# A round's result is spread one round later, the place matrix is built at the round's end, expert weights come in 16 KB pieces, router weights are loaded later

## The chip, the cores and the metric

One NeuronCore of a Trainium2 chip runs the whole program in one launch. The metric is the device time in microseconds of one execution. Three runs of the kernel before gave 1340.18, 1341.22 and 1343.46 us, median 1341.22. The profile is of the run of 1341.22 us, whose span from first to last instruction is 1339.4 us.

## The reference

One inference step of a two-layer decoder trunk, all in fp32, on 256 prompt tokens and 8 sample tokens (T = 264 columns in the kernel). Layer 0 mixes tokens by dilated window attention, layer 1 by causal pooling; each is followed by a mixture of experts, which is what the change is about:

```python
def moe_ffn(h, g_norm, wgr, bgr, wer, ber, wg, wu, wd):
    u = rms_norm(h, g_norm).reshape(n, d)                 # d = 1024
    gates = route(u, wgr, bgr, wer, ber)                  # (n, 16): 2 of 16 experts per token, others 0
    a = jnp.einsum('td,edf->tef', ub, wg)                 # f = 512
    c = jnp.einsum('td,edf->tef', ub, wu)
    hh = jax.nn.silu(a) * c * gb[:, :, None]
    return h + jnp.einsum('tef,efd->td', hh, wd)
```

`route` is a softmax over 4 groups, the best group, and the two best of its 4 experts. Beside this the program copies the three key and value caches (about 176 MB) from their input to their output tensors, shifted by one token, by DMAs from DRAM to DRAM.

## The kernel before

All activations lie transposed: `hT` and `uT` hold feature chunk k (8 of 128) on the partitions and 264 tokens along the row. SyncE (SP) issues the weight loads and the cache copies ("moves", about 1 MB each) in one order written by hand; a move goes wherever the order has room. ScalarE (ACT) and GpSimd (POOL) issue small loads and stores. All waits are written out as semaphores.

**Expert rounds.** The 16 experts are taken in pairs, 8 pairs a layer; a pair takes a round, or more where an expert has over 64 tokens (`CAP`). In this data each pair takes one, so there are 16 rounds. The bounds of the loop over rounds are read from `rounds_i` (L302) at each pair, in `all_rounds` (L301 to L307), by every engine. One round on TensorE (PE), in order:
- gather: 24 matmuls (L1180, two records each) of the token-major `u_tok` by the 0/1 matrix `pick` put the chosen tokens of both experts side by side into banks 0 and 1; DVE copies bank 0 (L928), ACT bank 1 (L708) into `u_slots`;
- place: 3 matmuls (L1187) of `pick_gate` (the same matrix times the gate) by the identity give the matrix that spreads slots back over tokens; ACT copies it to `place` (L710);
- gate and up: 64 matmul records (L1197), 32 against `ring_lo` (gate), then 32 against `region_a` (up); ACT takes Silu of bank 2 (L712), DVE multiplies by bank 3 (L931);
- turning: 4 transposes of `hid_rows` (L1202), copied by DVE (L933) and ACT (L714);
- down: L1213 into banks 4 and 5, copied by ACT into `y_pair` (L717);
- spread: 8 matmuls (L1222) of `y_pair` by `place` into four banks in turn, each added to `hT` by DVE (L936).

POOL makes `pick` (L561) and `pick_gate` (L559) in turn, 12 instructions, once the place matrix of the round before has been made (`place_made`).

**Weights.** Six slots of 2 MB (gate, up, down for either expert of a pair). SP reloads gate when the round's gate matmuls are done, up after up, then one move, down after down (`next_pair`, L418 on; `expert`, L382 to L386). The loads view a weight as `(k p) f -> p k f`: a partition gets 8 rows of 2 KB each for gate and up, 4 of 4 KB each for down.

**Router.** After the norm PE computes logits (L1144), turns `uT` into token-major banks (L1151), which DVE (L865) and ACT (L700) copy to `u_tok`; DVE then picks the experts. The router's weights are loaded by ACT (L631 to L634) at the end of the qkv stage; their semaphore `consts_landed` is the one on which PE (ahead of L1048) and DVE (ahead of L785) wait before the sample tokens' attention. After prompt attention ACT issues the pool mixer's loads (L682 to L686), and its next work is the norm's square (L285), once w_o's product has been added.

## Time and profile before

| what | value |
|---|---|
| median of the runs | 1341.22 us |
| the profiled execution | 1341.22 us, span 1339.4 us |
| PE busy | 1149.8 us, 86% |
| DVE, ACT, POOL busy | 31%, 17%, 17% |
| DMA, mean rate | 345 GB/s, 462.63 MB |
| mean granted TensorE clock | 0.908 of full |
| layer 0: first gather to last spread | 602.1 to 921.3 us |
| layer 1: the same | 1013.5 to 1332.0 us |

Times within the profile are from the first instruction. A granted clock of 1.00 is 2.4 GHz, of 0.50 is 1.2 GHz. An engine name with a q is that engine's sequencer: it waits, branches, reads registers or issues DMAs while the engine itself may be idle.

### The profile page before, as it was taken

To read this page: it belongs to the slowest core of one execution; us is meant where nothing else is said; L and a number is where in the kernel's file an instruction comes from. 1 tells how busy PE (TensorE), PEld (TensorE's weight loads), DVE (VectorE), ACT (ScalarE), POOL (GpSimd) and SP (SyncE) were. 2 spreads that over 40 slices of the span, in tenths; PEclk is the share of its full clock that TensorE was granted. 3 is DMA by queue.
4 is the path that set the end of the run, shared out by engine and by line. 5 is a ranking of instruction groups with operands and counts; after the bars stand their busy time and mean duration, and the time that the engine had idled before them with its cause. 6 is when DMAs were issued, how large, how long until landed. Compare 5 with 4: busy or idle time off the path is not lost.

```text
span 1339.4 us, 15976 instructions
## 1 busy us (share of the span) xinstructions
PE 1149.8 (86%) x5409; PEld 740.9 (55%) x5410; DVE 420.2 (31%) x821; ACT 224.1 (17%) x508; POOL 222.4 (17%) x466
## 2 busy tenths in 40 slices
PE   5998799999588999739988998997557899899888
PEld 3887688778424888635444444444344444444443
DVE  3456457546511663230111110114640111011112
ACT  1221122222100442110111111111011111111110
POOL 0014204204300120022211222100004022222100
PEclk9999899999777899857999999999655999999999
DMA  9999999998899988999999899899997998989997
GB/s 379 317 410 371 381 364 362 380 394 304 280 315 394 307 293 291 372 321 321 393 387 353 328 347 351 333 354 393 359 335 257 339 351 324 351 332 351 393 351 276
DMA packets 132562, 462.63 MB, mean 345 GB/s; under 512 B 12112, under 2 KB 20192, under 8 KB 129808
## 3 DMA queue, kind: packets, MB, share of 16 engines
q1 hardware_dynamic: 118768, 440.29, 89.3%
q0 software_dynamic: 5536, 18.88, 3.8%
q10 hardware_dynamic: 8232, 3.13, 1.0%
q8 instruction: 14, 0.23, 0.1%
q14 instruction: 12, 0.10, 0.0%
HBM read 455.19 MB, written 183.41 MB: 477 GB/s over the span
## 4 chain that ended last, share of the span: by engine, by line
PE 64%; DVE 9%; issue 5%; DMA 2%; ACT 2%; POOL 1%; ACTq 1%; DVEq 0%; POOLq 0%
PE bank L1197 17%; PE bank L1180 11%; PE bank L1213 8%; PE bank L1222 4%; PE bank L1023 4%; PE bank L1067 2%; PE bank L1135 2%; DMA out_dram<-scratch 1%; DVE ring_lo L775 1%; PE bank L1094 1%; PE bank L1187 1%; PE bank L1114 1%; PE bank L280 1%; PE bank L1102 1%; PE bank L1144 1%
## 5 line engine op out<-in xcount | busy, mean ns | idle before, releaser
L1023 PE MATMUL bank<-uT,ring_lo 128*128 128x264 f32 x1152 | 272.7, 391 | 8.5 <-DVE uT L293 6.0
L1023 PEld LDWEIGHTS bank<-uT,ring_lo 128*128 128x128 f32 x1152 | 217.2, 193 | 48.4 <-issue 9.7
L1180 PE MATMUL bank<-scratch 128*128 128x128 f32 (+1 forms) x768 | 149.2, 328 | 40.4 <-POOL scratch L561 24.8
L1180 PEld LDWEIGHTS bank<-scratch 128*128 128x128 f32 (+1 forms) x768 | 113.9, 204 | 78.5 <-issue 28.1
L1197 PE MATMUL bank<-ring_lo,scratch 128*64 128x512 f32 x512 | 124.9, 645 | 0.0
L1213 PE MATMUL bank<-ring_lo,scratch 128*64 128x512 f32 x512 | 113.4, 594 | 11.4 <-DVE scratch L933 11.4
L764 DVE RECIPROCAL scratch<-scratch 128x264 f32<-128x264 f32 x48 | 86.5, 1802 | 111.1 <-ACT scratch L611 111.1
L931 DVE TENSOR_TENSOR scratch<-bank,scratch 128x512 f32<-128x512 f32 x16 | 11.1, 691 | 327.9 <-PE bank L1197 327.9
L1197 PE MATMUL bank<-region_a,scratch 128*64 128x512 f32 x512 | 112.6, 592 | 0.0
L936 DVE TENSOR_TENSOR hT<-bank,hT 128x264 f32<-128x264 f32 x128 | 55.3, 432 | 129.7 <-PE bank L1222 128.3
L1213 PEld LDWEIGHTS bank<-ring_lo,scratch 128*64 128x64 f32 x512 | 42.3, 137 | 72.2 <-issue 72.2
L544 POOL TENSOR_TENSOR small<-epsc 128x1 f32<-128x1 f32 x65 | 12.5, 193 | 403.1 <-PE bank L1187 388.6
L1197 PEld LDWEIGHTS bank<-ring_lo,scratch 128*64 128x64 f32 x512 | 38.0, 147 | 73.2 <-issue 72.9
L1197 PEld LDWEIGHTS bank<-region_a,scratch 128*64 128x64 f32 x512 | 36.6, 137 | 73.2 <-issue 73.2
L1222 PE MATMUL bank<-scratch 128*128 128x264 f32 x256 | 61.2, 392 | 0.0
L1222 PEld LDWEIGHTS bank<-scratch 128*128 128x128 f32 x256 | 47.3, 190 | 20.3 <-issue 13.0
L481 POOL COPY region_a<-scratch 128x264 f32<-128x264 f32 x48 | 24.3, 506 | 195.3 <-DVE scratch L765 194.9
L559 POOL TENSOR_SCALAR scratch<-slot_no,scratch 128x64 f32<-128x64 f32 (+1 forms) x96 | 55.8, 582 | 0.7 <-issue 0.3
L775 DVE TENSOR_TENSOR ring_lo<-ring_lo,scratch 128x1024 f32<-128x1024 f32 x24 | 42.0, 1748 | 12.7 <-POOL scratch L473 8.7
L605 ACT ACTIVATE scratch<-bank 128x264 f32<-128x264 f32 x48 | 18.7, 390 | 157.8 <-PE bank L1023 157.8
L548 POOL COPY scratch<-scratch 128x6 f32 x16 | 3.0, 189 | 245.6 <-issue 245.6
L928 DVE COPY scratch<-bank 128x512 f32<-128x512 f32 x16 | 11.1, 691 | 102.3 <-PE bank L1180 102.3
(218 smaller groups left out, 1209.2 us busy)
## 6 DMA issues: line engine op xcount, KB each, us to landing
out_dram<-in_cache_kv_w_dram SPq DMA_DIRECT2D x128, 1023.5 KB, 17.3
ring_lo<-in_w_gate_dram SPq DMA_DIRECT2D x32, 2048.0 KB, 12.9
region_a<-in_w_up_dram SPq DMA_DIRECT2D x32, 2048.0 KB, 18.0
ring_lo<-in_w_down_dram SPq DMA_DIRECT2D x32, 2048.0 KB, 17.1
ring_lo<-in_w_qkv_dram SPq DMA_DIRECT2D x18, 2048.0 KB, 16.9
out_dram<-in_cache_kv_w_dram SPq DMA_DIRECT2D x32, 1022.0 KB, 32.8
ring_lo<-in_cache_kv_w_dram POOLq DMA_DIRECT2D x24, 512.0 KB, 10.6
ring_lo<-in_cache_kv_w_dram SPq DMA_DIRECT2D x6, 2048.0 KB, 13.9
```

What stands on the lines that cost most here:

```text
L481: nc.gpsimd.tensor_copy(qk[:, g, n // KT, n % KT, :], zn[:, n % 4, :]).then_inc(zn_kept, 1)
L559: nc.gpsimd.tensor_scalar(pick_gate[0:n, b, at], slot_no[0:n, :], pair_at[0:n, 0, b, e:e + 1], pair_at[0:n, 1, b, e:e + 1], ALU.is_equal, ...
L764: chain(vec.reciprocal(zri[:, n % 2, :], zr[:, n % 2, :]))
L775: chain(vec.tensor_tensor(k_tile, k_tile, q_rep[b % 2][:, :], ALU.mult))
L936: vec.tensor_tensor(hT[:, m, :], spread_bank[m % 4][:, 0:T], hT[:, m, :], ALU.add).then_inc(spread_added, 1)
L1023: last = mm(z_bank[s % 4][:, 0:T], w[:, k, at:at + P], uT[:, k, :], start=(k == 0), stop=(k == KT - 1))
L1067: last = mm(bank[3 + a][rows, :], p_masked[:, b % 2, g, rows], slot(g)[:, at:at + 512], start=(half == 0 and g == 0 and b % 2 == 0), stop= ...
L1135: last = mm(bank[m % 2][:, 0:T], w[:, f % 4, m * P:(m + 1) * P], oT[:, f, :], start=(f == 0), stop=(f == KT - 1))
L1180: last = mm(bank[m // 4][:, m % 4 * P:(m % 4 + 1) * P], u_tok[0:sizes[b], b, m * P:(m + 1) * P], pick[0:sizes[b], b, :], start=(b == 0), s ...
L1197: last = mm(bank[2 + w][rows, :], u_slots[:, k, rows], weights[e][w][:, k, :], start=(k == 0), stop=(k == KT - 1))
L1213: last = mm(bank[4 + a][rows, :], hid[:, f, rows], weights[e][2][:, f, a * 512:(a + 1) * 512], start=(f == 0), stop=(f == FT - 1))
L1222: mm(spread_bank[m % 4][:, 0:T], y_pair[:, m * P:(m + 1) * P], place, start=True, stop=True).then_inc(spread, 1)
```

## The change

- A round's `y_pair` and `place` are no longer spread at its end. The next round of the same layer spreads them: 4 spreads (m = 0 to 3) stand between up and turning, 4 between turning and down. DVE adds the first four between its multiply and its copy of the turned rows, the others behind that copy.
- Before a layer's first round DVE sets `y_pair` and `place` to zero (the first round then spreads zeros), and after the last round PE and DVE do one more spread of 8, for which both read the count of rounds (`all_of_layer`).
- The place matmuls stand at the end of the round, behind down, and wait for all eight additions; ACT copies `place` behind `y_pair`. Bank order for spreads is 6, 7, 2, 3.
- PE no longer waits for ACT's half of `u_slots` until half of the gate matmuls are issued.
- POOL makes all of `pick` first, as soon as the round before has gathered, and `pick_gate` once its place matrix is made; each has a semaphore of its own.
- Expert weights are viewed `(p k) f -> p (k f)`: one piece of 16 KB a partition. To match, `u_tok` is dealt out in the copies from PSUM (feature 8p+k goes to chunk k), and the transposes read every fourth column of `hid_rows`.
- The router's six loads stand behind prompt attention, ahead of the pool mixer's loads on ACT, with a semaphore of their own on which PE waits ahead of the logits.

```diff
+        def dealt(b, half, n):
+            return u_tok[0:n, b, :].rearrange("t (k p) -> t k p", k=KT)[:, :, half * HD:(half + 1) * HD]
-        spread_bank = [bank[n] for n in (2, 3, 6, 7)]
+        spread_bank = [bank[n] for n in (6, 7, 2, 3)]
-        N_CONSTS = 8 + 2 * LAYERS
+        N_CONSTS = 6
+        N_ROUTER = 2 + 2 * LAYERS
-        expert_w = (w_gate.rearrange("l e (k p) f -> (l e) p k f", p=P), ...
+        expert_w = tuple(w.rearrange("l e (a p k) f -> (l e) p a (k f)", a=1, p=P) for w in (w_gate, w_up, w_down))
+        def all_of_layer(eng, layer):
+            return eng.value_load(rounds_i[0:1, ds(layer * (NP + 1) + NP, 1)], min_val=NP, max_val=MAX_ROUNDS)
...
 POOL one_round
-                pool.wait_ge(place_made, q + 1)
+                pool.wait_ge(gathered, q * 2 + 2)
...
-                        nc.gpsimd.tensor_scalar(pick_gate[0:n, b, at], ...
                         last = nc.gpsimd.tensor_scalar(pick[0:n, b, at], ...
                 last.then_inc(pick_ready, 1)
+                pool.wait_ge(place_made, q + 1)
...
+                        last = nc.gpsimd.tensor_scalar(pick_gate[0:n, b, at], ...
+                last.then_inc(pick_gate_ready, 1)
...
 ACT, behind prompt attention (moved here from the end of the qkv stage)
+            for layer in range(LAYERS):
+                dma(wr[:, layer, :, 0:NG], router_group_w[layer].rearrange("(k p) g -> p k g", p=P)).then_inc(router_landed, 16)
+                dma(wr[:, layer, :, NG:], router_expert_w[layer].rearrange("(k p) g -> p k g", p=P)).then_inc(router_landed, 16)
+            dma(brow[:, :, 0:NG], ...).then_inc(router_landed, 16)
+            dma(brow[:, :, NG:], ...).then_inc(router_landed, 16)
...
 DVE
+                for a in range(2):
+                    vec.memset(y_pair[:, a * 512:(a + 1) * 512], 0.0).then_inc(y_copied, 1)
+                vec.memset(place, 0.0).then_inc(place_ready, 1)
...
-                    vec.tensor_copy(u_tok[0:n, b, 0:D // 2], bank[2 * b][0:n, :]).then_inc(u_tok_dve, 1)
+                    vec.tensor_copy(dealt(b, 0, n), bank[2 * b][0:n, :].rearrange("t (p k) -> t k p", k=KT)).then_inc(u_tok_dve, 1)
...
 PE one_round, behind the gather
                 pe.wait_ge(slots_dve, q + 1)
-                pe.wait_ge(slots_act, q + 1)
-                for b in range(3):
-                    last = mm(bank[6][:, b * P:b * P + sizes[b]], pick_gate[0:sizes[b], b, :], ...
...
+                        if w == 0 and k == KT // 2:
+                            pe.wait_ge(slots_act, q + 1)
...
+                pe.wait_ge(y_copied, q * 2 + 2 * (layer + 1))
+                pe.wait_ge(place_ready, q + (layer + 1))
+                for m in range(4):
+                    if m == 2:
+                        pe.wait_ge(silu_ready, q + 1)
+                        pe.wait_ge(hid_rows_ready, q + 1)
+                    spread_out(m)
                 pe.wait_ge(hid_rows_ready, q + 1)
                 for f in range(FT):
-                    last = nc.tensor.transpose(..., hid_rows[:, f * P:(f + 1) * P], ident[:])
+                    last = nc.tensor.transpose(..., hid_rows[:, f::FT], ident[:])
                 last.then_inc(hid_turned, 1)
+                for m in range(4, KT):
+                    pe.wait_ge(spread_added, q * KT + (layer * KT + m - 3))
+                    spread_out(m)
...
 behind down
-                pe.wait_ge(place_ready, q + 1)
-                for m in range(KT):
-                    ...
-                    mm(spread_bank[m % 4][:, 0:T], y_pair[:, m * P:(m + 1) * P], place, start=True, stop=True).then_inc(spread, 1)
+                pe.wait_ge(pick_gate_ready, q + 1)
+                pe.wait_ge(spread_added, q * KT + (layer + 1) * KT)
+                for b in range(3):
+                    last = mm(bank[6][:, b * P:b * P + sizes[b]], pick_gate[0:sizes[b], b, :], ...
+                last.then_inc(place_made, 1)
```

## Rows read from the trace of the kernel before

**Rows 1.** The page: busy us by engine; groups: busy us, mean ns | idle before.
```profile
PE 1149.8 (86%) x5409; PEld 740.9 (55%) x5410; DVE 420.2 (31%) x821; ACT 224.1 (17%) x508; POOL 222.4 (17%) x466
...
L936 DVE TENSOR_TENSOR hT<-bank,hT 128x264 f32<-128x264 f32 x128 | 55.3, 432 | 129.7 <-PE bank L1222 128.3
...
L559 POOL TENSOR_SCALAR scratch<-slot_no,scratch 128x64 f32<-128x64 f32 (+1 forms) x96 | 55.8, 582 | 0.7 <-issue 0.3
```
**Rows 2.** Chain of waits, one round: start us, us, what ended last.
```profile
727.37 8.52 PE bank L1180 x48
736.65 1.00 PE bank L1187 x6
737.65 15.61 PE bank L1197 x64
754.09 0.67 PE bank L1202 x4
754.79 0.43 DVE scratch L933
755.46 7.09 PE bank L1213 x32
762.55 3.76 PE bank L1222 x16
766.31 1.06 issue
```
**Rows 3.** Stretches of time: us, busy of PE, PEld, DVE, ACT, POOL, clock, DMA share, GB/s.
```profile
689.01:727.37 38.36, 34.89 (x171) 17.88 (x171) 5.27 (x11) 5.73 (x8) 7.23 (x19) 1.00 0.95 360
727.37:767.37 40.00, 36.58 (x171) 18.24 (x171) 5.27 (x11) 5.73 (x8) 7.23 (x19) 0.96 0.90 340
734.67:738.08 3.41, 2.63 (x18) 1.85 (x18) 0.00 (x0) 0.99 (x2) 0.29 (x2) 1.00 1.03 410
738.08:741.50 3.42, 3.42 (x12) 0.98 (x10) 0.00 (x0) 1.28 (x1) 3.42 (x8) 0.50 1.02 407
602.11:617.18 15.07, 15.05 (x48) 11.39 (x48) 0.69 (x1) 0.00 (x0) 1.18 (x6) 0.50 1.02 343
1013.51:1028.58 15.07, 15.06 (x48) 11.39 (x48) 0.69 (x1) 0.00 (x0) 1.16 (x6) 0.50 1.02 343
```
**Rows 4.** PE's sequencer at the loop's end, L307, 762 to 768 us.
```profile
L307 PEldq ALU_OP  x1: 32/32/32, 765.0 to 765.0; - x1
```
**Rows 5.** Chain of waits, first rounds' gate and up, layers 0 and 1.
```profile
619.66 15.10 PE bank L1197 x64
1031.06 15.90 PE bank L1197 x64
```
**Rows 6.** Timeline: PE at layer 0's start, with the idle time ahead of it.
```profile
602.11 15.05 PE L1180 MATMUL bank<-scratch 128*128 128x128 f32 x48 [12.70 <-POOL scratch L561]
```
**Rows 7.** Timeline from the qkv stage's end to the sample tokens' attention.
```profile
365.81 0.77 PE L1048 MATMUL bank<-bucket_s,tabrep 32*128 32x129 f32 x2 [12.22 <-DMA brow<-in_router_expert_b_dram]
365.08 0.95 POOL L518 COPY scratch<-region_a 128x384 f32<-128x384 f32 x2 [5.88 <-DMA out_dram<-scratch]
369.23 0.36 DVE L787 TENSOR_TENSOR scratch<-scratch 128x192 f32<-128x192 f32 x1 [2.57 <-DMA scratch<-qkv_of_samples]
```
**Rows 8.** DMA queues (packets, MB, share): 538:546 us ACT's, 356:358 ACT's, 548:551.4 SP's.
```profile
q10 hardware_dynamic: 94, 0.09, 3.7%
...
q10 hardware_dynamic: 2061, 0.08, 64.4%
...
q1 hardware_dynamic: 13, 0.00, 0.2%
```
**Rows 9.** ACT's timeline behind prompt attention.
```profile
551.88 1.96 ACT L285 ACTIVATE scratch<-hT 128x2112 f32<-128x2112 f32 x1 [29.30 <-DVE hT L854]
```
**Rows 10.** Stretches: only 4 KB pieces of down, then only 2 KB pieces.
```profile
733.00:743.00 10.00, 9.22 (x42) 4.64 (x42) 0.00 (x0) 2.27 (x3) 5.21 (x12) 0.83 1.01 404
753.00:765.00 12.00, 10.42 (x49) 5.25 (x48) 2.85 (x6) 2.24 (x4) 0.00 (x0) 1.00 1.05 388
```

More of the change, by code:

```diff
@@ L385, in expert @@
                 src = src[e] if isinstance(e, int) else src[ds(e, 1)].rearrange("a p k f -> p (a k) f")
-                sp.dma_start(slot(s).rearrange("p (k f) -> p k f", k=FT if what == 2 else KT), src).then_inc(ring_full[s], 16)
+                sp.dma_start(slot(s).rearrange("p (a f) -> p a f", a=1), src).then_inc(ring_full[s], 16)
             expert(0, 0, 0)
@@ L570, in _ @@
             carry(55).then_inc(place_made, 1)
+            for n in range(2):
+                carry(52 + n).then_inc(gathered, 1)
             for layer in range(LAYERS):
@@ L924, in router, with add_spread, one_round @@
                 vec.tensor_copy(rounds_i[0:1, layer * (NP + 1):(layer + 1) * (NP + 1)], rounds_f[0:1, layer, :]).then_inc(rounds_ready, 1)
-            def one_round(q, p):
-                dve.wait_ge(gathered, q * 2 + 1)
+            def add_spread(n, half):
+                for m in range(4 * half, 4 * half + 4):
+                    dve.wait_ge(spread, n * KT + (m + 1))
+                    vec.tensor_tensor(hT[:, m, :], spread_bank[m % 4][:, 0:T], hT[:, m, :], ALU.add).then_inc(spread_added, 1)
+            def one_round(q, layer):
+                dve.wait_ge(gathered, q * 2 + 3)
                 vec.tensor_copy(u_slots[:, 0:KT // 2, :], bank[0].rearrange("p (k n) -> p k n", n=P)).then_inc(slots_dve, 1)
@@ L931, in one_round @@
                 vec.tensor_tensor(hid_rows, bank[3][:, :], silu, ALU.mult).then_inc(hid_rows_ready, 1)
+                add_spread(q + layer, 0)
                 dve.wait_ge(hid_turned, q + 1)
                 vec.tensor_copy(hid[:, 0:2, :], bank[0][:, 0:2 * P].rearrange("p (f n) -> p f n", f=2)).then_inc(hid_dve, 1)
-                for m in range(KT):
-                    dve.wait_ge(spread, q * KT + (m + 1))
-                    vec.tensor_tensor(hT[:, m, :], spread_bank[m % 4][:, 0:T], hT[:, m, :], ALU.add).then_inc(spread_added, 1)
+                add_spread(q + layer, 1)
             def experts(layer):
                 dve.wait_ge(rounds_ready, layer + 1)
-                all_rounds(dve, layer, one_round)
+                all_rounds(dve, layer, lambda q, p: one_round(q, layer))
+                end = all_of_layer(dve, layer)
+                for half in range(2):
+                    add_spread(end + layer, half)
                 vec.memset(small[:, 62:63], 0.0).then_inc(layer_added, 1)
@@ L1139, in router @@
                 pe.wait_ge(u_ready, n_norm + 1)
+                pe.wait_ge(router_landed, 16 * N_ROUTER)
                 for b in range(3):
@@ L1169, in _, with spread_out @@
                         slot(c).rearrange("p (k f) -> p k f", k=FT)) for a, b, c in SLOTS]
+            def spread_out(m):
+                mm(spread_bank[m % 4][:, 0:T], y_pair[:, m * P:(m + 1) * P], place, start=True, stop=True).then_inc(spread, 1)
             def one_round(q, p, layer):
@@ L1215, in one_round @@
                     last.then_inc(y_half, 1)
-                pe.wait_ge(place_ready, q + 1)
-                for m in range(KT):
-                    if m % 4 == 0:
-                        pe.wait_ge(y_copied, q * 2 + (m // 4 + 1))
-                    if m >= 4:
-                        pe.wait_ge(spread_added, q * KT + (m - 3))
-                    mm(spread_bank[m % 4][:, 0:T], y_pair[:, m * P:(m + 1) * P], place, start=True, stop=True).then_inc(spread, 1)
+                pe.wait_ge(pick_gate_ready, q + 1)
+                pe.wait_ge(spread_added, q * KT + (layer + 1) * KT)
+                for b in range(3):
+                    last = mm(bank[6][:, b * P:b * P + sizes[b]], pick_gate[0:sizes[b], b, :], ident[0:sizes[b], 0:sizes[b]],
+                              start=True, stop=True)
+                last.then_inc(place_made, 1)
             def experts(layer):
                 all_rounds(pe, layer, lambda q, p: one_round(q, p, layer))
+                end = all_of_layer(pe, layer)
+                pe.wait_ge(y_copied, end * 2 + 2 * (layer + 1))
+                pe.wait_ge(place_ready, end + (layer + 1))
+                for m in range(KT):
+                    if m >= 4:
+                        pe.wait_ge(spread_added, end * KT + (layer * KT + m - 3))
+                    spread_out(m)
             norm_sums(pe, 1)
```

35 lines of the change are left out of this document (16 added, 19 removed).

## The prediction

> **What bounds the kernel now.** The page comes first: TensorE is busy 1149.8 us of 1339.4 [rows 1], every other engine a third or less (of the groups under it, DVE's eight additions a round cost 0.43 us each and POOL's `pick_gate` instructions 0.58). The chain of waits then shows that in the expert rounds nearly every step from gather to gather is PE's own [rows 2]. A round with the clock at full takes 38.36 us, one in which the clock falls once 40.00 [rows 3]; In a round PE stands still four times [rows 2]: 735.89 to 736.65, until ACT has copied its half of the slots (0.76 us); 753.26 to 754.09, until DVE has multiplied (0.83); 754.76 to 755.46, until the turned rows are copied (0.70); and 766.31 to 767.37, the loop's registers (1.06). No weight load ends a wait there. DMA is not idle, though: in these two rounds its share is 0.95 and 0.90, at 360 and 340 GB/s [rows 3].
>
> The reader should look hardest at the granted clock. Right behind the first gap and the place matmuls it fell: from 734.67 to 738.08 PE is busy 2.63 us of 3.41 and the clock is 1.00, from 738.08 to 741.50 it is 0.50 [rows 3]. That happened in 5 of the 14 rounds that are not a layer's first, each time at this place, never at the loop's gap. There the dense gate matmuls come next, and the clock is back at once: 15.61 us in place of the 13.93 that is left when 40.00 - 38.36 = 1.64 are taken off, the price of such a fall. A layer's first gather shows what a gather does at half clock: 15.07 us against 8.52, the clock at 0.50 from its first to its last matmul [rows 2, 3], and it came back only inside gate and up, which took 15.10 and 15.90 us [rows 5]. So gather doesn't bring the clock back, and gate does.
>
> **The change part by part.**
>
> Slots. Gate starts when DVE's half is there, which is copied during the second half of gather; ACT's copy lies beside the first half of gate, 3.5 us. The 0.76 us become some 0.04: 0.72 x 16 rounds = -11.5 us. Bounds: 0 and 0.76 a round.
>
> Turning. Before, from the end of up to the start of down: 755.46 - 753.26 = 2.20 us, and then spread, 3.76, behind down. After: spread m 0 and 1 take 0.94 us, longer than the 0.83 in which the multiply ends, so m 2 and 3 and the transposes (about 0.54 without the wait for the first) follow without a gap; DVE adds the first four (0.43 each [rows 1]) and copies the turned rows by about 3.1 us, while m 4 to 7 keep PE until 4.3. Down starts 4.3 us behind up, where 2.20 + 3.76 = 5.96 stood: -1.66 x 16 = -26.6 us. Bounds: 0 (all waits come back) and 1.66.
>
> The loop's gap. The sequencer began the loop's end at 765.0 [rows 4], while four spreads (two records each, 0.235 us a record) were still to run in part, and gather started at 767.37, 2.3 us later; 1.26 us of that lay under spread. Behind the change the last instructions are place's six, of which four cover only some 0.8 us, so the gap is about 1.5 us, not 1.06: +0.4 x 14 = +5.6 us. Bounds: 0 and +1.2 (nothing covered).
>
> The ends. Each layer gets one more spread (3.76) and the loop's exit ahead of it, about 1.5: +5.3 x 2 = +10.5 us. Where the place matrix took 1.72 us at half clock in a first round it now takes 1.00: -1.4 us for both.
>
> POOL. Ahead of the first gather PE waits for POOL, 12.70 us [rows 6]. Of the twelve instructions there six stay ahead of it: the six of `pick_gate` go, 0.58 apiece [rows 1], -3.5 x 2 = -7.0 us. POOL is idle four fifths of the time [rows 1], and `pick` is made a whole round early. The three memsets lie beside PE's logits.
>
> Attention. PE waited 12.22 us, until 365.8, for the router's last load [rows 7], DVE with it. Without it PE is done with these matmuls early, but DVE also waits for the token stores; POOL's wait for the same ones ended at 365.08 [rows 7], or some 1 us sooner once the router's packets no longer mix in. The sample rows land earlier too, as ACT no longer issues their loads behind the router's. So what stood at 369.23 [rows 7] starts at about 364.9: -4.5 us. Bounds: 0 (the stores are the last all the same) and 12.2 (PE's whole wait).
>
> 16 KB pieces. While only 4 KB pieces went, the 16 engines moved 404 GB/s at a share of 1.01; while only 2 KB pieces went, 388 at 1.05 [rows 10]: 400 against 370 at a share of 1. The 13.6 MB of a round need about 36 us as they are, and 33 to 34 with every piece large. No load is waited for now and none will be, for a round gets no shorter than 36: 0 us. Without the larger pieces this would be at its limit. Bounds: 0, and a few us a round should 16 KB be slower, for which no row speaks.
>
> The columns of `hid_rows` are read by every fourth. No row shows a strided read by PE. The four transposes take 0.67 us [rows 2]; the near end is nothing, the far end a doubling, 0.67 x 16 = 10.7 us. I take +2, the dealing copies with it, which lie mostly beside PE. The Trainium skill (SBUF — State Buffer, the DMA port swizzle section, its note on cachelines) says that accesses which each touch a new 16-byte line pay a penalty, and every fourth fp32 is just that; by it I would take the far end, and the sum would rise by some 9 us. No row bears on it.
>
> The router's loads stand ahead of the pool mixer's on ACT. ACT is idle 29.30 us there, until w_o's product is added at 551.9 [rows 9]. Beside SP's 64 KB pieces ACT's queue gets few packets through, 94 in 8 us, and the router has over 4,000 (1024 rows by 2 loads by 2 layers). But ahead of 551.4 SP's queue runs empty, 13 packets in 3.4 us; with nothing large beside them 2,061 such packets passed in 2 us [rows 8]. As SP's weights are through sooner, that gap grows to some 8 us. +1 us for ACT's lateness; bounds 0 and the rival below.
>
> The clock. Five falls go with the first gap: -1.64 x 5 = -8.2 us. But the place matmuls, among the sparsest work of a round, now stand right ahead of its longest gap, and behind the gap comes gather, also sparse. That is together 2.5 us with little in it, where 0.76 us of idling next to the place matmuls had been enough. I expect a fall in most rounds, and now at the head of gather, which then stays at half: up to 15.07 - 8.52 = 6.55 us, 5.4 where the fall comes a little into it, and gate begins at half too, 1.2 to 2.0 us (15.10 and 15.90 less 13.9 [rows 5]). So 7.0 us a fall. In 11 of 14 rounds: +77 us. Bounds: 0 and 14 x 8.3 = 116.
>
> Sum: -11.5 - 26.6 + 5.6 + 10.5 - 1.4 - 7.0 - 4.5 + 2 + 1 - 8.2 = -40 us without new falls, +77 with them: **+37 us**. The profiled execution is the median one, 1341.22 us for a span of 1339.4, so the changed kernel comes to 1378 us. A difference within 0.3%, 4 us, can't be told from none by timing this kernel.
>
> **The rivals.**
>
> *The clock holds (faster).* The loop's gap of 1.06 us cost no clock in 14 rounds [rows 2, 3], and what is in the changed one is only 1.5. Then only the savings are left: 1341 - 40 = 1301 us, or 1310 if as many falls as before stay at their old price. Against it: a gap of 0.76 did cost the clock. For it: the same gap did not in 9 of 14. The Trainium skill (TensorE: Matmul & The Clock Gate, HAM oscillation) warns of PE idling for far longer than either gap here, and by that rule this rival is the forecast; the falls in the trace disagree with it. The point that decides is 40 / 7 = 5.7: with six falls the change gives nothing, with fewer it is faster, with more it is slower.
>
> *A few falls.* Whether a fall comes depended on the round's position, since equal rounds differed. With 3 to 8 in place of 11: 1322 to 1357 us.
>
> *The router's packets get stuck (slower, or it eats the gain).* If they haven't gone by 551 us, SP's next 23 moves share the engines with them at about 12 packets a us [rows 8]. ACT is then held in its issues, and the norm, logits and everything behind wait. Each 12 packets left over cost 1 us: 500 would cost 42 us, 1343 us with the clock holding (1301 + 42) and 1420 with the falls (1378 + 42). For it: over 4,000 packets. Against: the gap at SP and the rate in it [rows 8].
>
> *Weights are late.* Only if 16 KB pieces run below 350 GB/s; each 10% below adds 4 us a round, some 60 in all: 1361 with the clock holding. The trend from 2 to 4 KB speaks against it.
>
> **How the numbers follow.** Falls in 9 to 14 rounds: 0.60, its own range 1355 to 1400 us. A few falls: 0.15, half of it slower, a third faster. The clock holds: 0.20, 1298 to 1318. Stuck packets or late weights: 0.05. The predicted time is 1378 us; the range 1308 to 1400 takes in most of the faster case. Faster 0.26, within 0.3% 0.05, slower 0.69.
>
> **What would show it.** Right: the granted clock at 0.50 over most gathers, a mean clock well below 0.908, gathers of 13 to 15 us, and PE's idle time between gather and gate, up and turning, and turning and down gone. Wrong: gathers of 8.52 us throughout, and rounds of some 36.5. The gap behind place should be 1.3 to 1.7 us. DVE's L787 should start near 365 us; ACT's square should follow w_o's last addition within 2 us, else the router's loads held ACT. The page should count a smaller number of packets and no wait of PE for `ring_full`.

## The result and the profile after

The changed kernel takes 1273.88 us (median of 4 runs, 1272.44 to 1276.9), the kernel before 1341.58 us beside it: a ratio of 0.9497, 95% interval 0.948 to 0.9515. The forecast was 1378 us, slower, with a range of 1308 to 1400. It was wrong in its sign. Times below are medians of all runs of a kernel; a ratio leaves out a run over 1.5% above its kernel's fastest (one, in the second test).

The page after, its line of busy times (us, share of the span, instructions); [rows 1] has the one of before:

```profile
PE 1142.9 (90%) x5441; PEld 736.3 (58%) x5442; DVE 428.3 (34%) x843; ACT 224.4 (18%) x508; POOL 225.1 (18%) x484
```

PE does almost the same work in a span of 1272.0 us, not 1339.4. Where its idle time went is seen in the chain of waits of one round after (start us, us, what ended last), beside [rows 2]:

```profile
674.36 8.44 PE bank L1214 x48
682.79 13.88 PE bank L1228 x64
696.68 2.08 PE bank L1203 x8
698.76 0.47 PE bank L1240 x4
699.23 1.78 PE bank L1203 x8
701.01 7.02 PE bank L1254 x32
708.03 0.95 PE bank L1260 x6
708.99 3.05 PE bank L1214 x17
```

L1214 is gather, L1228 gate and up, L1203 spread, L1240 turning, L1254 down, L1260 place. All eight lines are PE's and each starts where the one above ends. The last two lines are the point: place ends at 708.99 and the next round's gather starts at 708.99. The loop's gap, 1.06 us in [rows 2] and forecast to become 1.5, is not there (a line "issue", as there and below, is time in which the engine waits for nothing that the profile shows). The view of stretches shows it for a whole round, and the clock with it (us, busy of PE, PEld, DVE, ACT, POOL, granted clock, DMA share, GB/s), as [rows 3]:

```profile
674.36:708.99 34.63, 34.63 (x171) 17.39 (x171) 5.15 (x11) 5.73 (x8) 7.37 (x20) 1.00 1.00 427
593.91:608.97 15.06, 15.06 (x50) 11.47 (x52) 0.69 (x1) 0.00 (x0) 4.63 (x13) 0.50 0.96 322
```

PE is busy 34.63 us of 34.63 and the clock is 1.00. PE has no gap in any other round either, but for layer 0's second, where it stands still twice for weights (0.86 us for up's, 0.77 ahead of down), and the clock is 1.00 in every round but a layer's first. No gather but a layer's first ran at half clock. That first one still takes 15.06 us (second row), as before.

Why the gap is gone is seen at PE's sequencer, L316, the loop's end, within the same round (duration in ns, then start in us); [rows 4] is the same place before:

```profile
L316 PEldq ALU_OP  x1: 32/32/32, 704.5 to 704.5; - x1
L316 PEldq MOVE  x1: 29/29/29, 706.7 to 706.7; - x1
```

It starts on the loop's registers at 704.5, 3.5 us ahead of down's end, and is through at 706.8, 2.2 us ahead of the next gather. Before, it began at 765.0, with 1.3 us of spread left. What held it there is DVE's fourth addition of that round, for which the last spread waits (start us, us; it ends at 765.00):

```profile
764.57 0.43 DVE L936 TENSOR_TENSOR hT<-bank,hT 128x264 f32<-128x264 f32 x1
```

In the changed kernel the last of the eight additions is over long before the sequencer gets to the loop's end:

```profile
701.05 0.43 DVE L952 TENSOR_TENSOR hT<-bank,hT 128x264 f32<-128x264 f32 x1
```

The 67.4 us between the two spans, by stretches: 8.2 ahead of layer 0's first gather (602.11 to 593.91), 26.6 in layer 0 (first gather to last spread, 319.2 to 292.6), 3.5 between the layers, 29.0 in layer 1 (318.5 to 289.5).

### The profile page after: what moved, and what is told of

Its sections match the earlier page's. It is cut to its first block, busy times and chain, and to the rows that moved or that the text cites. A ratio compares the mean times of both kernels' runs of the same rounds, so it can differ in the third digit from the quotient of the medians.

```text
span 1272.0 us, 16186 instructions
## 1 busy us (share of the span) xinstructions
PE 1142.9 (90%) x5441; PEld 736.3 (58%) x5442; DVE 428.3 (34%) x843; ACT 224.4 (18%) x508; POOL 225.1 (18%) x484
## 4 chain that ended last, share of the span: by engine, by line
PE 59%; DVE 7%; issue 3%; DMA 3%; ACT 1%; POOL 1%; ACTq 1%; POOLq 0%; DVEq 0%; SPq 0%
PE bank L1228 17%; PE bank L1214 11%; PE bank L1254 8%; PE bank L1203 5%; PE bank L1165 2%; PE bank L1097 2%; DMA region_a<-in_w_up_dram 2%; PE bank L1124 1%; PE bank L1132 1%; PE bank L1144 1%; PE bank L1175 1%; PE bank L285 1%; PE bank L1260 1%; PE bank L1104 1%; PE bank L1121 1%
## 5 line engine op out<-in xcount | busy, mean ns | idle before, releaser
L1214 PE MATMUL bank<-scratch 128*128 128x128 f32 (+1 forms) x768 | 149.3, 328 | 18.0 <-POOL scratch L568 18.0
L1214 PEld LDWEIGHTS bank<-scratch 128*128 128x128 f32 (+1 forms) x768 | 113.9, 204 | 50.6 <-POOL scratch L568 18.2
L1228 PE MATMUL bank<-ring_lo,scratch 128*64 128x512 f32 x512 | 117.5, 613 | 0.0
L1254 PE MATMUL bank<-ring_lo,scratch 128*64 128x512 f32 x512 | 113.4, 595 | 0.8 <-issue 0.8
L1228 PE MATMUL bank<-region_a,scratch 128*64 128x512 f32 x512 | 112.6, 592 | 0.9 <-DMA region_a<-in_w_up_dram 0.9
L553 POOL TENSOR_TENSOR small<-epsc 128x1 f32<-128x1 f32 x83 | 16.0, 195 | 387.4 <-PE bank L1260 334.8
L1228 PEld LDWEIGHTS bank<-region_a,scratch 128*64 128x64 f32 x512 | 37.0, 137 | 73.9 <-issue 73.9
L1228 PEld LDWEIGHTS bank<-ring_lo,scratch 128*64 128x64 f32 x512 | 36.3, 141 | 69.2 <-issue 67.5
L1254 PEld LDWEIGHTS bank<-ring_lo,scratch 128*64 128x64 f32 x512 | 35.8, 137 | 69.9 <-issue 69.9
L1203 PE MATMUL bank<-scratch 128*128 128x264 f32 x288 | 73.2, 397 | 1.0 <-ACT scratch L736 1.0
L952 DVE TENSOR_TENSOR hT<-bank,hT 128x264 f32<-128x264 f32 x144 | 61.8, 432 | 20.7 <-PE bank L1203 17.5
L1203 PEld LDWEIGHTS bank<-scratch 128*128 128x128 f32 x288 | 50.8, 190 | 24.3 <-issue 17.0
L794 DVE TENSOR_TENSOR ring_lo<-ring_lo,scratch 128x1024 f32<-128x1024 f32 x24 | 42.0, 1749 | 11.5 <-POOL scratch L482 7.7
```

What stands on the lines that cost most here:

```text
L794: chain(vec.tensor_tensor(k_tile, k_tile, q_rep[b % 2][:, :], ALU.mult))
L952: vec.tensor_tensor(hT[:, m, :], spread_bank[m % 4][:, 0:T], hT[:, m, :], ALU.add).then_inc(spread_added, 1)
L1203: mm(spread_bank[m % 4][:, 0:T], y_pair[:, m * P:(m + 1) * P], place, start=True, stop=True).then_inc(spread, 1)
L1214: last = mm(bank[m // 4][:, m % 4 * P:(m % 4 + 1) * P], u_tok[0:sizes[b], b, m * P:(m + 1) * P], pick[0:sizes[b], b, :], start=(b == 0), s ...
L1228: last = mm(bank[2 + w][rows, :], u_slots[:, k, rows], weights[e][w][:, k, :], start=(k == 0), stop=(k == KT - 1))
L1254: last = mm(bank[4 + a][rows, :], hid[:, f, rows], weights[e][2][:, f, a * 512:(a + 1) * 512], start=(f == 0), stop=(f == FT - 1))
```

## The experiments

Gaps and falls below are read for the 14 rounds that are not a layer's first. A fall is a drop of the granted clock from 1.00 to 0.50 in such a round; it shows as a gather, or a gate and up, above its 8.5 or 13.95 us. They are counted in the one profiled run of each kernel. "Sparse" is said of gather and place, whose matmuls are of 128 columns, "dense" of gate, up, down and the added matmuls, of 512 or 264. The letters A, B, C are the theories of the expectation above each result.

**The forecast's arrangement made true.** Ahead of place PE waits until this round's result is copied:

```diff
                 pe.wait_ge(pick_gate_ready, q + 1)
+                pe.wait_ge(y_copied, q * 2 + 2 * (layer + 2))
                 pe.wait_ge(spread_added, q * KT + (layer + 1) * KT)
```

> This kernel makes the forecast's arrangement true: before the place matmuls PE waits until ACT has copied this round's second half of down's result, so the last instructions of a round wait late and the sequencer cannot run ahead to the loop's end. Theory A (the forecast was wrong only in what lets the sequencer run ahead; its clock term would have been right with the gap there): PE stands some 0.7 us behind down, place follows, then a loop gap of 1.3 to 1.6 us, 2.2 us a round in all, +31 us over 14 rounds, and on top a fall of the clock at the head of most gathers, about 7 us each: 1274 + 31 + 77 = 1382 us, gathers of 13 to 15 us. Theory B (the clock holds anyway beside gaps of this size, the forecast's clock term was wrong by itself): the same gaps, gathers of 8.5 us throughout, about 1305 us. Theory C (the loop's end costs nothing wherever the waits stand): a gap of 0.7 us behind down only, about 1284 us.

Measured: 1411.99 us, ratio 1.055 (1.0518 to 1.0582). The chain of one round of it:

```profile
721.64 0.61 ACT scratch L734
722.25 0.12 issue
722.37 1.02 PE bank L1261 x6
723.39 1.37 issue
724.76 14.13 PE bank L1214 x48
738.89 15.96 PE bank L1228 x64
```

PE's sequencer at the same loop end:

```profile
L316 PEldq ALU_OP  x1: 32/32/32, 722.4 to 722.4; - x1
```

And the stretches of its gather and of the whole round:

```profile
724.76:738.89 14.13, 14.13 (x50) 10.75 (x52) 0.69 (x1) 1.28 (x1) 3.42 (x11) 0.54 0.86 368
724.76:769.37 44.61, 42.46 (x170) 21.95 (x171) 5.15 (x11) 5.73 (x8) 7.42 (x21) 0.81 0.73 306
```

Theory A, and more of it than forecast. The sequencer comes to the loop's end only at 722.4, as place starts; place covers 1.0 us of it and 1.37 are left. Gather then runs at a clock of 0.54. It fell in 14 rounds of 14, and a round takes 44.6 us: 34.63, 2.1 of gaps and 7.8 for the clock (one, the second of layer 1, takes 46.2). One wait in another place makes the change slower than the kernel before.

**A gap behind place alone.** Only gather waits, for ACT's copy of the place matrix:

```diff
                 pe.wait_ge(pick_ready, q + 1)
+                pe.wait_ge(place_ready, q + (layer + 1))
```

> Here only gather waits, for ACT's copy of the place matrix of the round before; the last instructions of a round do not wait, so the sequencer meets the loop's end early and the gap is that of the copy alone, some 0.6 us behind place. Theory A (run-ahead hides the loop's end, and a gap behind the place matmuls can cost the clock): gap 0.5 to 0.7 us, no loop gap added, +9 us over 14 rounds, 1283 us if the clock holds; with falls as often as behind the old gap of 0.76 us (5 of 14), now priced at 7 us, 1318 us. Theory B (clock holds beside such gaps): 1283 us and gathers of 8.5 us. Theory C (the sequencer does not hide the loop's end behind a round of its own): gap above 1.2 us, 1295 us or more.

Measured: 1323.74 us (1315.22 to 1338.08), ratio 0.9861 (0.981 to 0.9912). The profiled run is the fastest, 1315.22. It has gaps of 0.57 us in layer 0 and 0.48 in layer 1, so no loop gap was added, and 5 falls of 14. A round with and one without a fall, and the gather of the former:

```profile
673.11:708.35 35.24, 34.67 (x170) 17.38 (x171) 5.15 (x11) 5.73 (x8) 7.41 (x21) 1.00 1.01 429
708.35:749.72 41.37, 40.79 (x170) 20.96 (x171) 5.15 (x11) 5.73 (x8) 7.42 (x21) 0.83 0.84 352
708.35:721.35 13.00, 13.00 (x50) 9.82 (x52) 0.69 (x1) 1.28 (x1) 4.22 (x12) 0.60 1.01 430
```

Theory A again: half a microsecond of idling at this place costs 6 us or more when it brings a fall, and equal gaps bring it only at times. The spread of the four runs fits a number of falls that differs from run to run: the mean clock is 0.889 in the fastest and 0.875 in the slowest.

**The same gap, longer.** ACT makes two copies more ahead of that of the place matrix:

```diff
                     ac.wait_ge(place_made, q + 2)
+                    nc.scalar.activation(silu[:, 0:T], bank[6][:, 0:T], ACT.Copy)
+                    nc.scalar.activation(silu[:, T:], bank[6][:, 0:512 - T], ACT.Copy)
...
+                pe.wait_ge(place_ready, q + (layer + 1))
```

> The changed kernel; gather waits for ACT's copy of the place matrix, ahead of which ACT now copies 512 columns of the same bank elsewhere (results unused). Nothing waits ahead of place, so this is the forecast's own arrangement: one gap of its size right behind the place matmuls. The copy alone gave a gap of 0.48 to 0.57 us and 5 falls in 14; the late place gave gaps of 0.77 and 1.37 us around the place matmuls and 14 falls in 14. Theory A (a gap of this size behind place costs the clock by itself): gap 1.2 to 1.5 us, falls in 11 to 14 of 14, gathers of 13 to 15 us, 8 us a fall: 1274 + 18 + 11..14 x 8 = 1380 to 1404 us. Theory B (it needed both gaps, ahead of place and behind it): about 5 falls, 1274 + 18 + 40 = 1332 us. Theory C (the clock holds behind one gap): 1292 us.

Measured: 1378.1 us (1362.17 to 1384.75), a little under theory A's 1380 to 1404. The profiled run took 1372.1; it has gaps of 1.12 us (layer 0) and 1.03 (layer 1) and 12 falls of 14:

```profile
674.88:710.68 35.80, 34.68 (x171) 17.39 (x171) 5.15 (x11) 6.28 (x10) 7.41 (x21) 1.00 1.00 428
710.68:752.59 41.91, 40.79 (x170) 21.01 (x171) 5.15 (x11) 6.28 (x10) 7.39 (x21) 0.84 0.84 349
```

Theory A: one gap is enough. The rounds with a fall are dearer by 6.1 us and by 7.7 in turn, 6.9 on the mean, where the forecast had 7.0, and 12 falls stand beside its 11. With a gap of some 1 us behind place the forecast's clock term comes out about as it was worked out. (Its gap was to be 1.5 us; none of that length was run behind place alone.)

**As long a gap, with dense work ahead of it.** Place goes ahead of down; gather waits for the copy of down's second half, which ACT delays by one copy:

```diff
+                pe.wait_ge(pick_gate_ready, q + 1)
+                pe.wait_ge(spread_added, q * KT + layer * KT + 5)
+                (the three place matmuls)
                 for e in range(2):
                     weights_there(SLOTS[e][2])
...
                 pe.wait_ge(pick_ready, q + 1)
+                pe.wait_ge(y_copied, q * 2 + 2 * (layer + 1))
```

> The changed kernel with place moved ahead of down, so that down, dense work, ends the round; gather waits for ACT's copy of down's second half, ahead of which ACT makes one more copy (result unused). So a gap as long as that of the last test stands ahead of gather, but no place matmuls next to it; the old loop gap of 1.06 us, behind the spreads, had just this surrounding and never cost the clock. Theory A (the clock falls where the gap lies between sparse matmuls on both sides): gap 1.1 to 1.3 us, no falls or a few, gathers of 8.5 us, 1274 + 14 x 1.2 = 1291 us. Theory B (the length of the gap decides, whatever stands beside it): 12 or more falls at 7 us each, about 1375 us.

Measured: 1320.34 us, ratio 0.9834 (0.98 to 0.9867). Gaps of 0.98 us in 14 rounds, 5 falls; one round with and one without:

```profile
746.67:782.16 35.49, 34.51 (x171) 17.48 (x171) 5.15 (x11) 6.01 (x9) 7.37 (x20) 1.00 0.93 386
782.16:823.76 41.60, 40.62 (x170) 21.02 (x170) 5.14 (x11) 6.01 (x9) 7.37 (x20) 0.84 0.79 328
```

Neither theory: fewer falls than with place at the gap (5 against 12), but not none. What stands next to the gap matters, as far as one profile each can tell, for this gap is also a little shorter (0.98 us, not 1.03 to 1.12); and it isn't all. The loop gaps of 1.05 to 1.15 us behind the eight spreads, in the kernel before and in two tests below that keep them, never cost the clock.

**A late wait that ends earlier.** The wait of the first test, for the other half of the result:

```diff
+                pe.wait_ge(y_copied, q * 2 + (2 * layer + 3))
```

> The changed kernel; ahead of place PE waits for ACT's copy of the first half of down's result, where the late-place test waited for the second. So there is a wait for this round's own work among the last instructions again, but one that ends some 2.7 us before down does. Theory A (the loop's end needs some 2.3 us of the sequencer, and whatever work of PE lies behind the last late wait covers it; late place had 0.96 us behind its wait and a gap of 1.36): 2.7 + 1.0 us lie behind this wait, so no gap, no falls, 1274 us. Theory B (any wait for the round's own work ahead of place holds the sequencer to the end): gap of 0.5 to 1.4 us and 5 to 14 falls, 1320 us or more. Theory C (a fixed number of matmuls is queued, the four records of the forecast): gap of 1.4 us, above 1370 us.

Measured: 1277.64 us, ratio 0.9522 (0.9502 to 0.9542). Its sequencer at the same loop end:

```profile
L316 PEldq ALU_OP  x1: 32/32/32, 710.0 to 710.0; - x1
```

And its chain there, down, place and the next gather:

```profile
705.60 7.02 PE bank L1254 x32
712.62 0.95 PE bank L1261 x6
713.57 2.53 PE bank L1214 x14
```

No gap in any steady round and no fall: theory A. The copy that PE waits for ends at 709.8, the sequencer is at the loop's end at 710.0, that needs 2.3 us and is through at 712.3, and gather is due at 713.57. So it is not the forecast's four queued records that cover the loop's end, but the work of PE that is left behind the last wait that ends late. The three kernels agree: 1.31 us behind the wait and a gap of 1.06 before; 1.0 and 1.37 in the first test; 3.6 and none here. What it lacks to the changed kernel, 3.8 us, lies elsewhere: layer 0 starts 1.9 us later, its second round waits 4.3 us for weights (1.6 there), and layer 1's first gate and up take 1.2 us more, less 1.9 us between the layers.

**The old order without its late waits.** The kernel before, with eight banks for the eight spreads:

```diff
-        spread_bank = [bank[n] for n in (2, 3, 6, 7)]
+        spread_bank = [bank[n] for n in (0, 1, 2, 3, 6, 7, 4, 5)]
...
+                pe.wait_ge(spread_added, q * KT + 1)      # ahead of gather
...
-                    if m >= 4:
-                        pe.wait_ge(spread_added, q * KT + (m - 3))
```

> The kernel before, with its order kept; only the eight spreads go to eight banks, so that none waits for an addition, and gather waits for the last addition instead. Theory A (it was the late waits within the spreads that held the sequencer back from the loop's end): the loop's end runs beside spread, and the gap ahead of gather falls from 1.06 us to what the last addition leaves, 0.5 to 0.8 us: 4 to 8 us less in all, 1333 to 1338 us. Theory C (the gap is the registers' own time, wherever the sequencer starts): 1.06 us or more stays, 1341 us or up to 8 us more. The falls of the clock at the gap ahead of gate stay, about 5 of 14, by either.

Measured: 1323.57 us, ratio 0.9879 (0.9859 to 0.99). Its sequencer (here L307):

```profile
L307 PEldq ALU_OP  x1: 32/32/32, 756.0 to 756.0; - x1
```

And the chain from spread to gather:

```profile
755.25 3.77 PE bank L1224 x16
...
759.04 0.44 DVE hT L938
...
759.53 2.49 PE bank L1183 x13
```

Theory A in its cause; the time is 10 us under its 1333 to 1338. The sequencer is at the loop's end at 756.0, at the head of spread (before, 1.3 us ahead of its end), and the gap is 0.53 us, that of DVE's last addition: 14 x 0.58 = 8 us. In this profile only 2 rounds had the fall in gate (5 before): 5 us. The rest, 4 us, lies ahead of layer 0 and between the layers, where nothing was changed.

**The gap ahead of gate, brought back.**

```diff
                 pe.wait_ge(slots_dve, q + 1)
+                pe.wait_ge(slots_act, q + 1)
```

> The changed kernel with the old gap ahead of gate: gate waits for ACT's half of the slots too. Place is no longer next to this gap. The gap itself costs 0.75 us in 16 rounds, +12 us, by every theory (the forecast had 0.72). Theory A (any gap of 0.76 us between sparse gather and gate lets the clock fall at times, and gate brings it back at once): 2 to 8 falls of 1.7 us, 1274 + 12 + 3..14 = 1289 to 1300 us, the falls at the head of gate, gathers of 8.5 us. Theory B (the falls of before needed the place matmuls next to the gap): no falls, 1286 us.

Measured: 1309.65 us, ratio 0.9792 (0.9754 to 0.983). The chain shows a longer gap than expected, from the end of gather at 756.63 to gate at 757.59:

```profile
748.18 8.45 PE bank L1214 x48
...
756.66 0.60 ACT scratch L727
757.26 0.33 issue
```

Stretches of a round without a fall and of this one:

```profile
675.35:711.02 35.67, 34.70 (x172) 17.54 (x171) 5.16 (x11) 5.73 (x8) 7.37 (x20) 1.00 1.00 425
748.11:785.43 37.32, 36.35 (x171) 17.76 (x171) 5.15 (x11) 5.73 (x8) 7.37 (x20) 0.95 0.88 365
```

Theory A in kind, too small in size: gaps of 0.97 us and 12 falls of 14, each 1.65 us, as gate brings the clock back. 16 x 0.97 + 12 x 1.65 = 35 us, and 36.5 were measured between the spans. Place need not be next to the gap.

**The old pieces in the new order.** The changed kernel with pieces of 2 and 4 KB, undealt copies and contiguous columns of `hid_rows`:

```diff
-        expert_w = tuple(w.rearrange("l e (a p k) f -> (l e) p a (k f)", a=1, p=P) for w in (w_gate, w_up, w_down))
+        expert_w = (w_gate.rearrange("l e (k p) f -> (l e) p k f", p=P), ...
```

> The changed kernel with its weights loaded in the old pieces of 2 and 4 KB (and with it the undealt copies and the contiguous columns of hid_rows). The forecast took the pieces as 0 us because it saw rounds of 36 us or longer; they now take 34.63 us. Theory A (the new order is so quick that the old pieces would limit it): PE waits for ring_full in most rounds, a round takes 35.5 to 36.8 us, 1274 + 14 x (0.9 to 2.2) = 1287 to 1305 us, perhaps with falls of the clock at these waits. Theory B (pieces give nothing even now): 1274 us, rounds of 34.6 us, no waits for weights. Theory D (the larger pieces themselves gave most of the 67 us): above 1320 us.

Measured: 1278.8 us, ratio 0.9546 (0.9527 to 0.9565). Rounds of 34.60 us with no wait for weights, but for layer 0's second, where PE waited 0.92 and 3.69 us and the clock fell (0.86 and 0.77 us in the changed kernel, no fall). Close to theory B: 4.9 us more than the changed kernel. That second round gives 4.7 of them; 1.2 are layer 1's first gate and up, which take as long in the test of the early wait with the large pieces, and 0.4 come off for the turning, 0.60 us a round and not the 0.63 with the strided columns. One steady round, in the view of stretches:

```profile
678.68:713.28 34.60, 34.60 (x172) 17.30 (x171) 5.16 (x11) 5.73 (x8) 7.37 (x20) 1.00 1.04 398
```

The DMA engines move 398 GB/s at a share of 1.04, where a round needs 393 (13.6 MB in 34.6 us); with the large pieces the same round moved 427 at 1.00. The old pieces keep up, with almost nothing to spare.

**The larger pieces in the old order**, the same edit the other way round:

> The kernel before with the larger pieces alone, and with them the dealt copies and the strided columns of hid_rows. The forecast gave the pieces 0 us and the strided reads +2. In the changed kernel the pieces were worth 5 us, all in the second round of layer 0, and the strided transposes cost 0.03 us a round. Theory A (no weight is waited for in the old order): 1339 to 1342 us, no difference above 0.3% but for the number of falls of the clock, 1.7 us each. Theory B (the pieces gave a good part of the 67 us): 1330 us or less.

Measured: 1348.43 us, ratio 1.0048 (1.003 to 1.0066). No gain, and a small loss, outside theory A's 1339 to 1342: the turning takes 0.75 us, not 0.66 (1.4 us in all), there were 7 falls, not 5 (3.4 us), and 1.2 us each were lost ahead of layer 0 and between the layers. Only the first of these is the edit's for certain.

**The router's loads alone**, moved in the kernel before from the end of the qkv stage to the end of attention:

```diff
-            for layer in range(LAYERS):
-                dma(wr[:, layer, :, 0:NG], ...).then_inc(consts_landed, 16)
...
             step(H // 4, 2, False, H + 2)
+            for layer in range(LAYERS):
+                dma(wr[:, layer, :, 0:NG], ...).then_inc(router_landed, 16)
```

> The kernel before with one part of the change alone: the router's loads move from ahead of the attention to its end. The forecast gave this part -4.5 us, bounds 0 and 12.2, and +1 us for ACT's lateness. The profile of the changed kernel puts 2.4 us at the attention's start, 3.6 and 5.2 us at two later marks. Theory A (the load's wait goes, DVE's wait for the token stores is next): 2.4 to 4.5 us less, 1336 us. Theory B (another wait takes its place in full): 1340 us. Theory C (the later marks are this part's as well): 5 us less or more.

Measured: 1335.91 us, ratio 0.9986 (0.9964 to 1.0007). By its time alone this can't be told from nothing. The profile (of a run of 1333.47 us, among the fastest of ten) says more: w_o's product starts at 516.54 us (522.63 before) and the first gather at 594.80 (602.11). PE's wait ahead of that gather stayed what it was in [rows 6], so POOL's part is another:

```profile
594.80 5.47 PE L1182 MATMUL bank<-scratch 128*128 128x128 f32 x17 [12.71 <-POOL scratch L562]
```

**Dense work ahead of a layer's first gather.** In the changed kernel, behind the position matmuls:

```diff
                 last.then_inc(positions_made, 1)
+                for k in range(14):
+                    mm(bank[7][:, 0:T], ones[:], uT[:, k % KT, :], start=(k == 0), stop=(k == 13))
```

> The changed kernel with 14 dense matmuls (128 rows, 264 columns, results unused) put behind the position matmuls of each layer, where PE waits some 9 us for POOL's pick. A layer's first gather starts at half clock and takes 15.06 us against 8.51, and its gate and up 16.6 and 15.4 against 13.95. Theory A (what PE did just before sets the clock of the first gather, and the wait hides the added work): first gathers of 8.5 to 10 us, 7 to 9 us less a layer, 1274 - 16 = 1258 us, down to 1256. Theory B (the clock comes back only after longer work than fits here): first gathers still about 15 us, 1274 us. Theory C (the added matmuls outlast POOL's wait): what is won is given back in part, 1262 to 1274 us.

Measured: 1262.97 us, ratio 0.9439 (0.9407 to 0.947). The timeline of PE at layer 0's start, the added matmuls and the first gather:

```profile
583.95 9.40 PE L1197 MATMUL bank<-uT,ones 128*128 128x264 f32 x28
593.34 8.51 PE L1216 MATMUL bank<-scratch 128*128 128x128 f32 x48
```

Stretches: the added matmuls, the second round of layer 0, the first of layer 1:

```profile
583.95:593.34 9.39, 9.39 (x30) 7.23 (x29) 2.85 (x19) 1.28 (x1) 3.33 (x11) 0.69 0.96 313
627.97:674.58 46.61, 36.59 (x171) 18.51 (x170) 5.16 (x11) 5.73 (x8) 7.39 (x20) 0.89 0.97 410
975.75:1010.27 34.52, 34.52 (x171) 17.28 (x170) 5.15 (x11) 4.06 (x6) 7.10 (x19) 1.00 0.90 342
```

The clock comes back inside the added matmuls, which end as POOL's wait does, and both first gathers take 8.5 us or less: theory A for the clock. (The time lies where theory C had it too, but the added matmuls outlast POOL's wait by 0.2 us at most.) Layer 1's first round is 34.5 us (42.7 before the edit). Layer 0 won nothing, for a reason that no theory named: its second round now waited 8.12 us for gate's weights, 1.15 for up's and 0.75 ahead of down, and its third started at 674.6, as without the edit.

**The moves that stand ahead of those weights.**

```diff
-            for n in range(PIECES[1]):
+            for n in range(3):
                 move(1, 1, n)                  # likewise for b = 2 to 6, and for b = 7 at the end
...
-                next_pair(p + NP, rounds_at(1, p), [(2, 7, p + 7)])
+                next_pair(p + NP, rounds_at(1, p), [(2, 7, p + 7), (1, p, 3)])
```

> The kernel with the 14 added matmuls, in which layer 0's second round then waited 8.1, 1.2 and 0.8 us for its gate, up and down weights. Here seven of SP's 1 MB moves of the cache, six from ahead of layer 0's second weights and one from the end, go into the rounds of layer 1, one each. Theory A (those weights were late because they queue behind the moves, 2.9 us each): the waits go, layer 0 is 8 to 10 us shorter, layer 1 keeps its 34.6 us rounds as they have some 3 us of DMA to spare: 1263 - 9 = 1254 us. Theory B (the engines are simply full; the bytes come back as waits in layer 1's rounds): 1258 to 1266 us.

Measured: 1254.6 us, ratio 0.9351 (0.9333 to 0.9368), the fastest of all kernels here. The second round of layer 0 and of layer 1:

```profile
630.66:665.29 34.63, 34.63 (x171) 17.39 (x171) 5.15 (x11) 5.73 (x8) 7.41 (x20) 1.00 1.01 431
999.33:1033.96 34.63, 34.63 (x171) 17.39 (x170) 5.15 (x11) 5.73 (x8) 7.37 (x20) 1.00 1.00 418
```

Theory A: all sixteen rounds now run without a wait, and the seven moves lie in layer 1's rounds at no cost.

## Why the prediction was wrong, point by point

The step that failed is "The loop's gap", priced at +0.4 us a round. It took the loop's end as something that is hidden by the last four queued records, whatever they are. What the runs show in its place: the sequencer issues ahead of PE where no wait holds it, and is at the loop's end 3.5 us ahead of down's end in the changed kernel. In the old order the last four spreads each waited for an addition of the same round (`spread_added`), and the fourth of these ended at 765.00, so it was held till 1.3 us before the end. The change took these waits out of the round's tail: `pick_gate_ready` and `spread_added`, ahead of place, are met at 678.0 and 701.5. (From 701.5 to 704.5 no wait of the program holds the sequencer, with 24 matmul records of down and place still to finish at 704.5; what bounds its lead there is not shown.) Taking them out of the old order shows the same (gap 1.06 to 0.53 us), a wait put back in the new order with 1.0 us of work behind it brings the gap back (1.37 us), and one with 3.6 us behind it does not. The term was -1.1 x 14 = -15 us, not +6. [Rows 4] already had the sequencer's start; what was not asked is which wait it came out of. The sum had slips too, none of which decides: four of place's six records cover 0.67 us by [rows 2], not 0.8; 1.31 us of the loop's end lay under spread, not 1.26; 15.61 - 1.64 is 13.97, not 13.93 (a round without a fall has 13.91); and 9 falls at 7.0 us come to 1364 us, not 1355.

The clock's +77 us hung on that gap and went with it: 0 falls in 14. By itself it stands: 12 falls of 14 at 6.9 us where a gap of 1.03 to 1.12 us was put behind place, 11 of 14 at 7.0 in the forecast; and 14 of 14 with the late wait. That the count comes so near is luck in part: with a gap half as long it was 5, and the profile is of one run. The rival "the clock holds" gave 1301 us and named the right sign for the wrong reason: behind place the clock doesn't hold beside such gaps; there was none. The rule of the Trainium skill named there (TensorE: Matmul & The Clock Gate, HAM oscillation), by which gaps of this length would be harmless, disagrees with these runs.

The other terms, forecast and measured:

| term | forecast, us | measured, us |
|---|---|---|
| slots | -11.5 | -12.5 (0.78 x 16) |
| turning | -26.6 | -26.1 (5.96 to 4.33, x 16) |
| ends of the layers | +10.5 | +8.6 (0.46 and 3.84, x 2) |
| place in the first rounds | -1.4 | -1.5 (1.72 to 0.97, x 2) |
| POOL's instructions | -7.0 | -6.8 (12.70 to 9.32 [rows 6], both layers) |
| attention's start, ACT | -3.5 | -4.8 (-8.2 ahead of the first gather, 3.4 of it POOL's; of the rest 1.6 are the norm's matmuls at a clock of 1.00, 0.70 before) |
| old falls | -8.2 | -8.2 (none is left) |
| strided and dealt reads | +2 | about 0 to +1 |
| pieces | 0 | 0 in steady rounds (old pieces in the new order: +4.7 in layer 0's second) |
| not in the forecast | | -3.6: gather, place, gate and up, and down together some 0.23 us shorter a round in the chain, where the gaps ahead of them are gone; +1.6: waits in layer 0's second round; +0.9: the first rounds' gate and up |
| loop's gap | +5.6 | -15.4 |
| new falls | +77 | 0 |

These make -67 us. All but the last two rows come to -45.7 in the forecast and to about -52 measured.

Attention. The mechanism was right: PE's wait of 12.22 us is gone, and what takes its place is DVE's wait for the token stores (engine timeline, with the idle time ahead of it and what ended it), the two rows that stand where [rows 7] had 369.23:

```profile
364.07 0.70 DVE L804 MEMSET scratch<- 128x768 f32 x1 [12.27 <-DMA out_dram<-scratch]
366.50 1.01 DVE L806 TENSOR_TENSOR scratch<-scratch 128x192 f32<-128x192 f32 x1 [1.73 <-DMA scratch<-qkv_of_samples]
```

The forecast was 364.9. In two profiles the part gave -3.6 and -6.1 us at the start of w_o's product. That start varies, though: 520.4 to 523.6 us in the three kernels with the old loads, 514.4 to 521.1 in the eleven with the moved ones. On the mean it is 3.8 us earlier, and no single pair of profiles gives the size. Clear of this are the norm's matmuls behind it: 3.83 us at a clock of 1.00 in all eleven, 5.43 to 5.51 at 0.70 in the three; why is not shown.

The router's packets did hold ACT, but ended in time. ACT's queue issues, and its next work:

```profile
519.64 17.10 ACTq L695 DMA_DIRECT2D wr<-in_router_group_w_dram  x1
536.77 3.46 ACTq L696 DMA_DIRECT2D wr<-in_router_expert_w_dram  x1
...
548.29 1.96 ACT L290 ACTIVATE scratch<-hT 128x2112 f32<-128x2112 f32 x1 [29.30 <-DVE hT L873]
```

The last issue of ACT ended at 545.4 and the square was due at 548.29: 2.9 us to spare, and not the +1 us taken.

The pieces: 0 us was right for steady rounds, and for the wrong reason. It rested on rounds of 36 us or more; rounds took 34.6. The old pieces keep up with those too, because they move 398 GB/s at a share of 1.04; to divide by the share, as was done with [rows 10], made the limit too low. In the new order they did cost 4.7 us, in layer 0's second round.

## What to carry to other kernels

In these kernels the loop's end is free if the engine still has as much issued work as its registers take (2.3 us here) when the last wait that ends late is over; so look, at the tail of the body, for waits on this iteration's own results, move them forward or give them another buffer, and read the time at which the sequencer reaches the loop's end. On TensorE an idle half microsecond next to sparse matmuls can cost ten times its length through the clock, and most where another sparse stage follows. Once PE's gaps are closed, look whether weights that were early enough stand behind copies in their queue.

## What the runs showed of the hardware

- Falls of the clock, by gap (14 rounds a kernel): 0.48 to 0.57 us behind place, ahead of gather, 5; 1.03 to 1.12 us there, 12; 0.98 us between down and gather, 5; 0.97 us between gather and gate, 12; 0.78 us between gather and place, 5, 2, 6 and 7 in four kernels; 0.77 us ahead of place and 1.34 to 1.38 behind it, 14; 0.52 to 1.15 us between spread and gather, 0 in 56 rounds of four kernels; no gap, 0 in every steady round of five kernels. What tells these apart is not settled: sparse work next to the gap goes with more falls, and the same gap brings one in one round and none in the next.
- What a fall costs depends on what follows it: 1.4 to 1.7 us when it is gate; 6.1 to 7.8 us, and 9.4 once, when it is gather.
- A transpose of every fourth fp32 column costs little: 0.63 us for four against 0.60 in the new order, 0.75 against 0.66 in the old. The forecast cited a penalty for accesses that each touch a new line from the Trainium skill (SBUF — State Buffer, the DMA port swizzle section). Its own far end for that, a doubling, was 0.67 us a round; 0.03 and 0.09 were measured.
